# First linear stage of a hybrid diffusion layer: chunk by chunk between sliced adaLN products

## The chip, the cores and the metric
The kernel runs on one core of a Trainium2 chip. The metric is the device time of one execution in microseconds (us). Three runs of the kernel before gave 2493.56, 2496.89 and 2493.85 us, median 2493.85 us.

## The reference
Two layers over 512 latent tokens and 256 context tokens, width 1024, all in float32. Each layer computes, with `c` and `c_ctx` as the two conditions (c is for latent rows, c_ctx for context rows):

```python
mods = split(silu(c) @ w_ada[l] + b_ada[l], 6)        # sh1, sc1, g1, sh2, sc2, g2
h = layernorm(x) * (1 + sc1) + sh1                      # "modulate"
y = token_mixers(h @ w_in[l])                           # attention A, attention B, Fourier C; gates
x = layernorm(ALPHA * x + g1 * y, ln1_g[l], ln1_b[l])
f = swiglu(layernorm(x) * (1 + sc2) + sh2)
x = layernorm(ALPHA * x + g2 * f, ln2_g[l], ln2_b[l])
```

In branch C the columns `uc = h @ w_in[:, uc part]` (512 features) go through a two-dimensional Fourier transform: over the 128 channels of a group, then over the positions.

## The kernel before, in words
The four big engines and the DMA queue of SyncE (SP) run one instruction list each; semaphores order them. The work is a list of phases, written out by `plan()`: first_norm, modulate, fourier_in, then per layer tokens_a, fourier, merge_c, attention (branch A), merge_a, values, attention (branch B), merge_b, and the channel mixer. Every engine walks the phases in this order. Weights come as a stream of units of 512 KB (128 partitions x 1024 columns), double buffered: SP loads a unit in two halves into `raw` (L417) when GpSimd has finished with the unit two before, ScalarE copies it to `w_hi` in a reduced-precision form (L587, `split`), GpSimd subtracts to get `w_lo` (L513, `lo_part`), and TensorE multiplies three terms, w_lo x h_hi, w_hi x h_lo and w_hi x h_hi.

- **first_norm.** SP loads `w_first` (the first 18 x 128 columns of w_ada of layer 0) in eight row blocks of 1152 KB into two buffers (L494). ScalarE's queue loads x (L666), the last two tiles after TensorE has used the first block. TensorE multiplies the conditions with each block (L1717), all eight accumulate in banks 0 to 4; then the rows are copied out (L679) and turned into columns (L1724). VectorE sums x (L1259), finds the inverse root of each of the six token tiles by a chain of eleven small steps (L1155 to L1166), and with ScalarE normalises x into `xn_first` (L1236, L631). When the products are complete and biased (L1110), `mods` for the first modulation are there.
- **modulate.** For each of 8 feature chunks TensorE transposes six tiles of 128 tokens (L1774, two banks each, four chunks in flight), ScalarE scales and shifts (L650), ScalarE or VectorE makes `h_hi` (L656, L1250), VectorE makes `h_lo` (L1244).
- **fourier_in.** Four units, one for 128 output features each, contract all 8 chunks at a time (L1745, L1747); ScalarE copies the result to `u_cols` (L694).
- **tokens_a.** Queries, keys and values of branch A, tokens on the partitions (L1830).
- **fourier.** TensorE multiplies `u_cols` with the channel DFT (L1888) in 12 pieces, ScalarE copies each to `z_sb` (L797). `z_sb` lies over `rope` and over the buffers of the adaLN units, so the first copy waits for `rope_step` (the table `rope_g` is made, L1296) and for `ada_used` of 42 units. Then the position DFT (L1901, L1905), with `mix` made by VectorE (L1355), which afterwards rotates q and k (`rotate`, L1316 to L1339).
- **merge_c.** Twelve units of gates and branch weights; VectorE multiplies a pair of chunks (L1380) after each three units.

The rest of the adaLN columns are made by VectorE in units of 128 columns: SP loads one (512 KB, L425, three buffers, each reload waits until VectorE has used the unit three before), and VectorE runs two multiply-and-sum products of 128x1024 (L1104), one for each condition; a copy of the conditions is loaded first (L430). `ADA_WINDOWS` puts units 18 to 41 ahead of tokens_a (they run beside fourier_in and tokens_a) and 42 to 47 in values; units 48 to 95 run beside the channel mixer. SP has one queue: a load that waits for VectorE holds up the weight loads behind it.

Of the kernel before, what the change touches and what calls it, by code (L numbers as in the profile page):

```python
# [65 lines left out]
ADA_WINDOWS = {("fourier_in", 0): (18, 42), ("values", 0): (42, 48)}  # L66
# [4 lines left out]
ADA_FIRST = 18  # L71
# [105 lines left out]
def increments(ph):  # L177

    t, k = ph.tiles, ph.kind
    if k == "first_norm":  # L180
        return {"loaded": 16 * t, "summed_x": t, "mean_ready": t, "squared": t, "norm_step": SECOND_ROOT * t, "root_ready": t,
                "normed": t // 2, "normed_odd": t // 2}
    if k == "modulate":
        return {"turned": KD, "h_val": KD, "h_hi": KD // 2, "h_hi_odd": KD // 2, "h_lo": KD}
# [18 lines left out]
    if k == "fourier_in":  # L203
        return {"evacuated": 4}
# [25 lines left out]
def build(nc, x_in, ctx_in, cond, cond_cols, w_first, w_ada, b_ada, stream, qk_gain, norm_rows, bias, ident_in,  # L230
# [21 lines left out]
    h_lo = sb("h_lo", [P, KD, TOK], F32R)  # L252
    acc = sb("acc", [P, KD, TOK])
# [71 lines left out]
    ada_at = {"fourier_in": 60, "values": 80, "gate_up": 72}  # L325
    ada_raw = {k: sb(f"ada_raw_{k}", [P, ADA_SLOTS, D], at=R + a * K) for k, a in ada_at.items()}
    ada_cond = {k: sb(f"ada_cond_{k}", [P, 2, D], at=R + (a + 12) * K) for k, a in ada_at.items()}
    ada_unused = {k: sb(f"ada_unused_{k}", [P, D], mybir.dt.bfloat16, at=R + (a + 20) * K) for k, a in ada_at.items()}


    first_raw = sb("first_raw", [P, 2, ADA_FIRST * P], at=R)
    first_rows = sb("first_rows", [2, ADA_FIRST * P], at=R + 48 * K)
    cond_act = sb("cond_act", [P, KD, 2], at=R + 58 * K)
    cond_rows = sb("cond_rows", [2, D], at=R + 60 * K)
# [44 lines left out]
    first_ready = [nc.alloc_semaphore(f"first_ready{s}") for s in range(2)]  # L379
# [27 lines left out]
    with block:  # L407

        @block.sync
        def _(sp):  # L410
# [49 lines left out]
            def window(ph, u):  # L460

                first, end = ADA_WINDOWS[ph.kind, 0]
                step = u - ph.unit - 4
                if step == 0:
                    if ph.kind == "fourier_in":
                        sp.wait_ge(S("h_lo"), KD)
# [3 lines left out]
                for part in (step - 1, step):  # L470
                    n = first + ADA_SLOTS * part
                    if step % 2 == 0 and part >= 0 and n < end:
                        load_ada(ph.kind, n, ADA_SLOTS)
# [15 lines left out]
            sp.dma_start(cond_act[:, :, :], cond_cols[:, :, :]).then_inc(S("cond_loaded"), 16)  # L489
            for k in range(KD):  # L490
                if k >= 2:

                    sp.wait_ge(S("first_used"), k - 1)
                sp.dma_start(first_raw[:, k % 2, :], w_first[k, :, :]).then_inc(first_ready[k % 2], 16)  # L494
            for u in range(n_units):
                for ph in phases:
                    if ph.kind == "bridge":
                        load_rows(ph, u)
                    elif (ph.kind, ph.layer) in ADA_WINDOWS:
# [3 lines left out]
                load_unit(u)  # L503
# [67 lines left out]
        def _(act):  # L571
            prime(act, ("gated", "projected", "silu", "evacuated"))
            consts = [(ident[:, :], ident_in[:, :]),
                      (ada_bias[:, :], b_ada[:, :]), (dft_c[:, :], dft_ch[:, :])]
            act.dma_start(cond_rows[:, :], cond[:, :]).then_inc(S("cond_loaded"), 16)
            act.wait_ge(S("cond_loaded"), 32)
# [81 lines left out]
            def rows_of_input(t):  # L658
# [432 lines left out]
        def _(dve):  # L1091
# [186 lines left out]
            def modulate(ph):  # L1278
                parts_of_h(ph, 0)
# [1235 lines left out]
```

## Time and profile before
| | us |
|---|---|
| median of three runs | 2493.85 |
| the profiled execution | 2498.33 |
| its span (first to last instruction) | 2496.5 |
| TensorE busy | 2315.2 (93%) |
| VectorE busy | 1222.7 (49%) |
| ScalarE busy | 949.3 (38%) |
| GpSimd busy | 1088.3 (44%) |

Matmul ends are modelled, so busy TensorE is not TensorE at its peak. The mean granted clock of TensorE was 0.978 of 2.4 GHz. DMA moved 263.86 MB, 106 GB/s in the mean, 244 GB/s in the first fortieth of the span.

### The profile page before, as it was taken

How to read it: one execution, taken by the hardware profiler on the slowest of the kernel's cores; microseconds unless marked ns; L12 is line 12 of the kernel's file. 1: busy time of each engine (PE TensorE's matmuls, PEld its weight loads, DVE VectorE, ACT ScalarE, POOL GpSimd, SP SyncE). 2: the span in 40 equal slices, each digit the busy share in tenths (PEclk: the TensorE clock that was granted, in tenths of full speed). 3: DMA queues.
4: the chain of work that ended last, by engine and by line, in shares of the span. 5: the costliest groups of instructions: out<-in, count | busy, mean ns of one | idle time of the engine just before them, and what ended most of it. 6: DMA issues, size and time to landing. Idle time of an engine off the chain costs nothing. (4 is left out here: it accounts for less than half of the span.)

```text
span 2496.5 us, 34770 instructions
## 1 busy us (share of the span) xinstructions
PE 2315.2 (93%) x13090; PEld 2107.2 (84%) x13090; DVE 1222.7 (49%) x2548; ACT 949.3 (38%) x1852; POOL 1088.3 (44%) x844
## 2 busy tenths in 40 slices
PE   6989999998899989999999979899998898999997
PEld 2879888987789989999999868778877788988887
DVE  5786266565543474663831274546635526311124
ACT  3222366435541562111111244256535536422223
POOL 1333255434443544333532433446434456644545
PEclk9989999999999999999999989999999999999999
DMA  6541100132112535443522533121222245533335
GB/s 244 193 139 51 51 26 26 43 137 58 58 45 74 181 130 190 134 154 107 171 90 67 161 101 122 54 64 35 65 67 66 66 152 161 152 94 99 110 117 170
DMA packets 117935, 263.86 MB, mean 106 GB/s; under 512 B 13348, under 2 KB 13604, under 8 KB 116136
## 3 DMA queue, kind: packets, MB, share of 16 engines
q1 hardware_dynamic: 108000, 233.89, 29.6%
q10 hardware_dynamic: 9800, 28.19, 3.4%
q8 instruction: 82, 1.34, 0.2%
q14 instruction: 53, 0.43, 0.1%
HBM read 251.53 MB, written 10.49 MB: 105 GB/s over the span
## 5 line engine op out<-in xcount | busy, mean ns | idle before, releaser
L513 POOL TENSOR_TENSOR w_lo<-raw,w_hi 128x512 fp32r<-128x512 f32 x632 | 864.8, 1390 | 1031.2 <-ACT w_hi L587 1030.6
L587 ACT ACTIVATE w_hi<-raw 128x512 fp32r<-128x512 f32 x632 | 366.8, 626 | 682.8 <-PE ps L1747 251.1
L525 POOL TENSOR_TENSOR p_sb<-p_sb,row_inv 128x768 f32<-128x768 f32 (+2 forms) x160 | 185.3, 1168 | 300.7 <-DVE row_inv L1486 300.0
L1745 PE MATMUL ps<-h_hi,w_lo 128*128 128x384 f32 (+1 forms) x864 | 311.4, 360 | 1.2 <-DVE h_lo L1244 1.2
L1745 PE MATMUL ps<-h_lo,w_hi 128*128 128x384 f32 (+1 forms) x864 | 311.1, 360 | 0.0
L1745 PE MATMUL ps<-h_hi,w_hi 128*128 128x384 f32 (+1 forms) x864 | 311.1, 360 | 0.0
L1576 DVE TENSOR_TENSOR ps<-silu_g,ps 128x768 f32<-128x768 f32 (+3 forms) x52 | 37.8, 726 | 379.4 <-PE ps L1747 177.5
L1745 PEld LDWEIGHTS ps<-h_hi,w_lo 128*128 128x128 f32 x864 | 162.2, 188 | 17.3 <-DVE h_lo L1244 1.4
L1745 PEld LDWEIGHTS ps<-h_lo,w_hi 128*128 128x128 f32 x864 | 162.2, 188 | 16.0
L1745 PEld LDWEIGHTS ps<-h_hi,w_hi 128*128 128x128 f32 x864 | 162.2, 188 | 15.9
L2091 PE MATMUL ps<-h_hi,w_lo 128*128 128x384 f32 (+1 forms) x408 | 134.3, 364 | 27.1 <-DVE k_ll L1431 14.8
L1747 PE MATMUL ps<-h_hi,w_hi 128*128 128x384 f32 x456 | 152.3, 334 | 0.0
L1747 PE MATMUL ps<-h_lo,w_hi 128*128 128x384 f32 x456 | 152.3, 334 | 0.0
L1747 PE MATMUL ps<-h_hi,w_lo 128*128 128x384 f32 x456 | 152.3, 334 | 0.0
L870 ACT ACTIVATE pt_hi<-ps 128x512 fp32r<-128x512 f32 (+1 forms) x208 | 114.3, 550 | 97.7 <-PE ps L2036 96.3
L1104 DVE SCALAR_TENSOR_TENSOR ada_unused_gate_up<-ada_raw_gate_up,ada_cond_gate_up 128x1024 bf16<-128x1024 f32 x96 | 143.2, 1491 | 5.3 <-DMA ada_raw_gate_up<-in_w_ada 0.3
L1493 DVE TENSOR_TENSOR pt_lo<-ps,pt_hi 128x512 fp32r<-128x512 f32 (+1 forms) x208 | 129.5, 624 | 21.6 <-ACT pt_hi L870 20.3
L862 ACT ACTIVATE p_sb<-ps,neg_max 128x768 f32<-128x768 f32 (+2 forms) x160 | 120.4, 753 | 35.6 <-DVE neg_max L1479 19.1
L2091 PE MATMUL ps<-h_lo,w_hi 128*128 128x384 f32 (+1 forms) x408 | 132.0, 359 | 0.0
L2091 PE MATMUL ps<-h_hi,w_hi 128*128 128x384 f32 (+1 forms) x408 | 131.9, 358 | 0.0
L2036 PE MATMUL ps<-ident,p_sb 128*128 128x128 f32 x736 | 108.8, 280 | 20.2 <-DVE pt_lo L1493 16.7
L2036 PEld LDWEIGHTS ps<-ident,p_sb 128*128 128x128 f32 x736 | 84.8, 141 | 42.8 <-DVE pt_lo L1493 36.3
(219 smaller groups left out, 5474.4 us busy)
## 6 DMA issues: line engine op xcount, KB each, us to landing
raw<-in_stream SPq DMA_DIRECT2D x632, 256.0 KB, 2.8
ada_raw_gate_up<-in_w_ada SPq DMA_DIRECT2D x48, 512.0 KB, 3.6
ada_raw_fourier_in<-in_w_ada SPq DMA_DIRECT2D x24, 512.0 KB, 4.4
bias_sb<-in_bias ACTq DMA_DIRECT2D x32, 320.0 KB, 3.0
first_raw<-in_w_first SPq DMA_DIRECT2D x8, 1152.0 KB, 5.2
scratch<-xr ACTq DMA_DIRECT2D x16, 512.0 KB, 3.8
xr<-scratch SPq DMA_DIRECT2D x14, 512.0 KB, 4.9
ln_rows<-in_norm_rows SPq DMA_DIRECT2D x8, 512.0 KB, 5.2
```

The lines of the kernel that those rows point to most:

```text
L513: nc.gpsimd.tensor_tensor(w_lo[:, u % 2, cols], raw[:, u % 2, cols], w_hi[:, u % 2, cols].bitcast(F32), ALU.subtract).then_inc(S("lo_made" ...
L525: nc.gpsimd.tensor_tensor(p, p, row_inv[:, c:c + 1].broadcast_to([P, keys]), ALU.mult).then_inc(S("p_ready"), 1)
L587: nc.scalar.activation(w_hi[:, s, cols], raw[:, s, cols], ACT.Copy).then_inc(S("hi_made"), 1)
L862: nc.scalar.activation(p_sb[branch][n % 2][i][:, 0:keys], region(branch, i, 0, keys), ACT.Exp, bias=neg_max[:, i:i + 1], accum_out=row_sum ...
L870: nc.scalar.activation(pt_hi[branch][:, a:a + w], ps[:, TURN_BANK[branch] + order % 2, 0:w], ACT.Copy).then_inc(S("hi_out"), 1)
L1104: nc.vector.scalar_tensor_tensor(ada_unused[kind][:, :], ada_raw[kind][:, s, :], 1.0, ada_cond[kind][:, c, :], ALU.mult, ALU.mult, accum_o ...
L1493: nc.vector.tensor_tensor(pt_lo[branch][:, a:a + w], ps[:, TURN_BANK[branch] + order % 2, 0:w], pt_hi[branch][:, a:a + w].bitcast(F32), AL ...
L1576: nc.vector.tensor_tensor(up, shaped(silu_g[:, c, 0:w]), up, ALU.mult).then_inc(S("hidden"), 1)
L1745: last = nc.tensor.matmul(bank(0), tile, x[:, k, 0:split], start=start, stop=stop)
L1747: last = nc.tensor.matmul(bank(1), tile, x[:, k, HALF:TOK], start=start, stop=stop)
L2036: last = nc.tensor.transpose(ps[:, TURN_BANK[branch] + order % 2, col:col + P], p_sb[branch][n % 2][i][:, a:a + P], ident[:, :])
L2091: last = nc.tensor.matmul(ps[:, bank, 0:b - a], tile, x[:, k, a:b], start=r == 0, stop=r == FILL_STEPS - 1, skip_group_check=True)
```

## The change
- w_first has 16 x 128 columns (shift and scale only) and is laid out in eight slices, one for each feature chunk k: the whole contraction for its 256 columns, 1 MB each, each with a buffer of its own. SP issues x first, then the slices, with weight units 0 and 1 behind slices 1 and 2. The small constants go ahead on ScalarE's queue; the gain is loaded in tokens_a.
- VectorE sums each tile of x as it lands and makes one inverse root for all six tiles.
- Three slices of products are made before x is turned, the fourth behind chunk 0's transposes, the other four inside fourier_in, behind chunks 0 to 3.
- fourier_in goes chunk by chunk: its units hold two chunks x 512 features; for every chunk it adds to six banks (four of 512 latent columns, two with 2 x 256 context columns); the transposes of the next chunk stand ahead of and in the middle of its matmuls, in banks 6 and 7, latent and context apart. All evacuations come at the end.
- The 32 adaLN units 16 to 47: 16 in tokens_a (4 ahead of rope_g, 12 behind it), 16 in merge_c (4, 6 and 6 behind its first three pairs), none in values. SP's loads for them stand ahead of single units, by `ADA_LOADS`. Buffers for tokens_a lie in `acc`, for merge_c in the region of the tables.

```diff
-ADA_WINDOWS = {("fourier_in", 0): (18, 42), ("values", 0): (42, 48)}
+ADA_WINDOWS = {"tokens_a": (16, 32), "merge_c": (32, 48)}
+ADA_LOADS = {"tokens_a": {2: 3, 3: 3, 4: 3, 5: 3, 6: 3, 7: 1}, "merge_c": {3: 3, 7: 2, 8: 3, 9: 2, 10: 3, 11: 3}}
+ADA_AFTER_PAIR = (4, 6, 6, 0)
...
-ADA_FIRST = 18
+ADA_FIRST = 2 * KD
+FIRST_AHEAD = 3
...
@@ sync, window(ph, u)
+                loads = ADA_LOADS[ph.kind]
+                step = u - ph.unit
+                if step not in loads:
+                    return
+                if step == min(loads):
+                    if ph.kind == "tokens_a":
+                        sp.wait_ge(S("first_mods"), KD)
                     else:
-                        sp.wait_ge(S("merged"), at(ph, "merged"))
+                        sp.wait_ge(S("mixed"), at(ph, "mixed"))
                     load_cond(ph.kind)
...
+            for t in range(ALLT):
+                src = x_in[t * P:(t + 1) * P, :] if t < LT else ctx_in[(t - LT) * P:(t - LT + 1) * P, :]
+                sp.dma_start(xr[:, t, :], src).then_inc(x_ready[t], 16)
             for k in range(KD):
-                if k >= 2:
-
-                    sp.wait_ge(S("first_used"), k - 1)
-                sp.dma_start(first_raw[:, k % 2, :], w_first[k, :, :]).then_inc(first_ready[k % 2], 16)
+                sp.dma_start(first_raw[k][:, :, :].rearrange("p a b -> p (a b)"), w_first[k, :, :]).then_inc(first_ready[k], 16)
+                if k in (1, 2):
+                    load_unit(k - 1)
...
@@ scalar
             def first_norm(ph):
                 squares(ph, 0, 1)
-                applied(ph, 0)
+                for i in range(0, ALLT, 2):
+                    first_row_out(i // 2)
+                    act.wait_ge(S("root_ready"), at(ph, "root_ready") + 1)
+                    nc.scalar.activation(xn_first[:, i, :], xr[:, i, :], ACT.Identity, scale=inv_s[:, ALLT + i:ALLT + i + 1],
+                                         bias=shift_s[:, i:i + 1]).then_inc(S("normed"), 1)
                 for s in range(2):
                     split(s, s)
...
             def fourier_in(ph):
+                for j in (2, 3):
+                    unit_done(ph.unit + j, j % 2)
+                for c in range(KB):
+                    nc.scalar.activation(u_cols[:, c, 0:LAT], ps[:, c, :], ACT.Copy).then_inc(S("evacuated"), 1)
...
-                        act.wait_ge(S("ada_used"), PRIME - ADA_FIRST + ADA_WINDOWS["fourier_in", 0][1])
...
@@ vector, merge_c
+                for c in range(KD):
+                    pair(acc[:, c, 0:w], c, 3 * (c // 2) + 3)
+                    if c % 2 and not ph.layer:
+                        ada_units(ph.kind, n, n + ADA_AFTER_PAIR[c // 2])
+                        n += ADA_AFTER_PAIR[c // 2]
...
@@ tensor
+            def first_products(k):
+
+                pe.wait_ge(first_ready[k], 16)
+                if k > FIRST_AHEAD:
+                    pe.wait_ge(S("h_lo"), 2 * (k - FIRST_AHEAD) + 2)
+                for j in range(KD):
+                    last = nc.tensor.matmul(first_sums(k), cond_act[:, j, :], first_raw[k][:, j, :], start=j == 0, stop=j == KD - 1)
+                last.then_inc(S("first_used"), 1)
...
             def fourier_in(ph):
...
+                for k in range(KD):
+                    if k + 1 < KD:
+                        turn_first(k + 1, 0)
+                    if 0 < k < KD - FIRST_AHEAD:
+                        first_turned(FIRST_AHEAD + k)
...
+                    u, kk = ph.unit + k // 2, k % 2
+                    weights_ready(u, kk * 512)
+                    pe.wait_ge(S("h_lo"), 2 * k + 2)
+                    for c in range(KB):
+                        if c == KB // 2 and k + 1 < KD:
...
+                            turn_first(k + 1, 1)
+                        tile = slice(512 * kk + P * c, 512 * kk + P * c + P)
+                        for name in TERMS:
+                            w, x = term(name, u % 2, h_hi, h_lo)
...
+                            nc.tensor.matmul(ps[:, c, :], w[:, u % 2, tile], x[:, k, 0:LAT], start=start, stop=stop, skip_group_check=True)
+                            last = nc.tensor.matmul(ps[:, KB + c // 2, CTX * (c % 2):CTX * (c % 2) + CTX], w[:, u % 2, tile], x[:, k, LAT:TOK],
+                                                    start=start and c % 2 == 0, stop=stop, skip_group_check=True)
+                    if kk:
+                        last.then_inc(S("unit_done"), 1)
+                    if FIRST_AHEAD + 1 + k < KD:
+                        first_products(FIRST_AHEAD + 1 + k)
```

## Rows read from the trace of the kernel before

**Rows 1.** The page, part 1: busy time, share of the span, instructions
```profile
PE 2315.2 (93%) x13090; PEld 2107.2 (84%) x13090; DVE 1222.7 (49%) x2548; ACT 949.3 (38%) x1852; POOL 1088.3 (44%) x844
```
**Rows 2.** TensorE's waits, 66 to 520 us: total, times, longest
```profile
PE ps L1888 <- ACT z_sb L797: 10.5, 1, 10.5
```
**Rows 3.** Timeline of TensorE, 0 to 66 us: start, length, line, count
```profile
6.53 9.99 PE L1717 MATMUL ps<-first_raw,cond_act 128*2 128x512 f32 x20 [6.53 <-DMA first_raw<-in_w_first]
19.24 4.03 PE L1717 MATMUL ps<-first_raw,cond_act 128*2 128x512 f32 x10 [2.72 <-DMA first_raw<-in_w_first]
...
55.39 4.35 PE L1774 MATMUL ps<-ident,xn_first 128*128 128x128 f32 x24 [1.50 <-DVE mods L1110]
60.32 1.87 PE L1774 MATMUL ps<-ident,xn_first 128*128 128x128 f32 x12 [0.58 <-DVE h_lo L1244]
```
**Rows 4.** Windows by stage: length, busy us by engine, clock, DMA share, GB/s
```profile
66.40:100.00 33.60, 33.53 (x193) 33.53 (x194) 20.56 (x25) 8.60 (x15) 12.09 (x6) 1.00 0.48 173
99.90:151.10 51.20, 50.40 (x290) 44.39 (x289) 45.26 (x63) 10.16 (x18) 20.54 (x11) 1.00 0.68 233
150.90:175.10 24.20, 13.69 (x51) 11.20 (x50) 22.41 (x33) 10.17 (x28) 8.98 (x4) 0.72 0.36 125
...
193.20:293.40 100.20, 100.13 (x579) 99.81 (x577) 38.99 (x72) 22.95 (x36) 33.48 (x24) 1.00 0.19 58
```
**Rows 5.** Timelines of TensorE and ScalarE in the channel DFT
```profile
150.89 7.07 PE L1888 MATMUL ps<-dft_c,u_cols 128*128 128x256 f32 x32
...
167.82 5.07 ACT L797 ACTIVATE z_sb<-ps 128x512 f32<-128x512 f32 x10 [12.21 <-issue]
```
**Rows 6.** Timeline of VectorE, 167 to 231 us
```profile
167.77 0.82 DVE L1305 TENSOR_TENSOR rope_t<-tok_a 128x640 f32<-128x640 f32 x1
...
178.28 0.96 DVE L1309 TENSOR_TENSOR v_a<-v_raw,v_a 128x768 fp32r<-128x768 f32 x1
...
229.01 1.82 DVE L1380 TENSOR_TENSOR acc<-gate_c,ps 128x768 f32 x2 [0.44 <-DVE tok_a L1339]
```
**Rows 7.** Windows of the start, columns as in rows 4
```profile
5.00:10.00 5.00, 3.47 (x5) 0.61 (x6) 0.00 (x0) 0.00 (x0) 0.00 (x0) 1.00 0.98 408
...
56.00:58.00 2.00, 2.00 (x12) 2.00 (x11) 0.00 (x0) 0.99 (x2) 0.00 (x0) 0.50 0.44 133
...
60.00:62.00 2.00, 1.55 (x12) 1.27 (x12) 1.82 (x3) 2.00 (x5) 0.00 (x0) 1.00 0.00 0
```
**Rows 8.** VectorE's groups by form, 6 to 66 us: busy, mean ns, idle before
```profile
L1160 DVE TENSOR_SCALAR tmp_s<-std_s,var_s 128x1 f32<-128x1 f32 x18 | 4.9, 273 | 0.7
...
L1250 DVE CAST h_hi<-ps 128x768 fp32r<-128x768 f32 x3 | 2.9, 957 | 3.3 <-ACT ps L650 3.0
```
**Rows 9.** ScalarE's groups by form, 6 to 66 us
```profile
L650 ACT ACTIVATE ps<-ps,mods 128x512 f32<-128x512 f32 x6 | 4.5, 752 | 4.7 <-PE ps L1774 4.7
L631 ACT ACTIVATE xn_first<-xr,shift_s,inv_s 128x1024 f32<-128x1024 f32 x3 | 3.7, 1235 | 5.4 <-DVE shift_s L1166 5.4
L650 ACT ACTIVATE ps<-ps,mods 128x256 f32<-128x256 f32 x6 | 3.2, 540 | 0.0
```
**Rows 10.** Timeline of SP's queue, 66 to 300 us: issues
```profile
88.95 14.10 SPq L425 DMA_DIRECT2D ada_raw_fourier_in<-in_w_ada  x6
```
**Rows 11.** The adaLN products of the first window: min/median/max ns, first and last start
```profile
L1104 DVE SCALAR_TENSOR_TENSOR ada_unused_fourier_in<-ada_raw_fourier_in,ada_cond_fourier_in x48: 1224/1226/2229, 76.6 to 164.1; 128x1024 bf16<-128x1024 f32 x48
...
  DMA ada_raw_fourier_in<-in_w_ada: 13.6, 6
```
**Rows 12.** VectorE's groups, 512 to 536 us (values)
```profile
L1104 DVE SCALAR_TENSOR_TENSOR ada_unused_values<-ada_raw_values,ada_cond_values 128x1024 bf16<-128x1024 f32 x12 | 17.5, 1455 | 7.6 <-DMA ada_raw_values<-in_w_ada 5.6 <-DVE ada_unused_values L1104 1.1
```
**Rows 13.** Tile raw, 193 to 293 us: from issue to landing
```profile
DMA to landing us min/median/max: 2.5/2.6/2.9
```
**Rows 14.** The subtractions to w_lo, 76 to 166 us, columns as in rows 11
```profile
L513 POOL TENSOR_TENSOR w_lo<-raw,w_hi x20: 1291/2248/2357, 76.7 to 157.8; 128x512 fp32r<-128x512 f32 x20
```
**Rows 15.** Window of the adaLN products in values, columns as in rows 4
```profile
512.30:535.30 23.00, 23.00 (x107) 19.41 (x106) 17.61 (x25) 5.08 (x8) 9.89 (x6) 1.00 0.44 156
```

More of the change, by code:

```diff
@@ L460, in window @@
             def window(ph, u):
[L462 to L466, printed above, removed]
+                loads = ADA_LOADS[ph.kind]
[5 more added lines that the diff above has]
+                        sp.wait_ge(S("first_mods"), KD)
                     else:
-                        sp.wait_ge(S("merged"), at(ph, "merged"))
+                        sp.wait_ge(S("mixed"), at(ph, "mixed"))
                     load_cond(ph.kind)
[L470 to L473, printed above, removed]
+                n = ADA_WINDOWS[ph.kind][0] + sum(count for other, count in loads.items() if other < step)
+                load_ada(ph.kind, n, loads[step])
             def beside(ph, u):
@@ new lines, in first_norm @@
+                step = chain("norm_step", at(ph, "norm_step"))
+                var, root, tmp, inv = (x[:, ALLT:2 * ALLT] for x in (var_s, std_s, tmp_s, inv_s))
+                dve.wait_ge(S("squared"), at(ph, "squared") + ALLT)
+                step(nc.vector.tensor_scalar(var, square_s[:, 1, :], 1.0 / D, EPS, ALU.mult, ALU.add))
+                step(nc.vector.tensor_scalar(tmp.bitcast(I32), var.bitcast(I32), 1, None, ALU.logical_shift_right))
+                step(nc.vector.tensor_scalar(inv.bitcast(I32), tmp.bitcast(I32), -1.0, ROOT_SEED, ALU.mult, ALU.add))
@@ new lines, in first_norm @@
+                for turn in range(3):
+                    step(nc.vector.scalar_tensor_tensor(tmp, inv, -0.5, inv, ALU.mult, ALU.mult))
+                    step(nc.vector.tensor_tensor(tmp, tmp, var, ALU.mult))
+                    step(nc.vector.scalar_tensor_tensor(inv, tmp, 1.5, inv, ALU.add, ALU.mult))
+                dve.wait_ge(S("mean_ready"), at(ph, "mean_ready") + ALLT)
+                nc.vector.tensor_tensor(shift_s[:, :], neg_mean[:, 1, :], inv, ALU.mult).then_inc(S("root_ready"), 1)
@@ L1290, in tokens_a @@
                     dve.wait_ge(S("stored"), at(ph, "stored"))
+                else:
+                    dve.wait_ge(S("cond_loaded"), 16 * 3)
+                    first, end = ADA_WINDOWS[ph.kind]
+                    ada_units(ph.kind, first, first + 4)
+                    dve.wait_ge(S("gain_loaded"), 16)
                 step = chain("rope_step", at(ph, "rope_step"))
@@ L1299, in tokens_a @@
                 step(last)
+                if not ph.layer:
+                    ada_units(ph.kind, first + 4, end)
+                    ada_biased(first, end, 1)
                 dve.wait_ge(S("evacuated"), at(ph, "evacuated") + ph.tiles + ALLT)
```

252 lines of the change are left out of this document (128 added, 124 removed).

## The prediction, on record before the change was run
> **What bounds the kernel now.** I read the page's totals first: TensorE is busy 93% of the span [rows 1], so a change gains only where TensorE stands still or where its work is not dense. The chain that ended last reaches back 27 us only and says nothing of the start. The waits of TensorE behind the first stage, to 520 us, hold one large entry: 10.5 us at L1888, the channel DFT, for ScalarE's copies to z_sb [rows 2]. The timeline of the first 66 us shows TensorE doing adaLN products at the pace of their transfers, some transposes, and no dense work before 66.5 us [rows 3]. The stages by windows [rows 4]: fourier_in to 100.0 us, tokens_a to 151.05, the DFT over channels to 175.05 (the position DFT behind it starts there), merge_c from 193.2 to 293.3. The window 150.9:175.1 is the hole: 24.2 us with 13.7 busy and a clock of 0.72, because the z_sb copies start at 167.82 [rows 5], after VectorE has worked off 24 adaLN units (the last product starts at 164.1, [rows 11]) and built rope_g (done ahead of 167.77, [rows 6]).
>
> So two places can pay: the 66.5 us ahead of fourier_in, and that hole.
>
> **The start.** Before, first_norm needs all of w_first (9.4 MB) ahead of any mods. Now x goes first, then slices of 1 MB. 5:10 moved 408 GB/s [rows 7]. With about 1 MB moved by 5 us, the 3.4 MB of x and constants are in at about 11 us and seen at 12; slice 0 is seen at 14.5, slice 1 at 17, slice 2 (unit 0 ahead of it) at 21, slice 3 (unit 1) at 24.7, the rest each 2.6 us later.
> Roots: of the six chains one is left, on six columns: thirteen steps of at most 0.27 us and 0.04 between [rows 8], 3 to 4 us. x summed at 14.6, squared at 16, root at 19. That is not the limit; the products are. Ten matmul records of a 2304-column row took 4.03 us at the full clock, while the first twenty took 9.99 [rows 3], about 5 us of them at half pace. A slice is 8 x 256 columns: 4.03 x 2048/2304 = 3.6 us, the first 6. So slice 0 ends at 20.5, 1 at 24.1, 2 at 27.7. ScalarE takes its three normalised tiles between the row copies, each behind first_used, so the last one (1.24 us, [rows 9]) ends at 29.4, though the root was there at 19. Transposes of chunk 0 to 31.1; slice 3 to 34.7; fourier_in proper begins at 35.5.
>
> Each chunk k then costs TensorE: matmuls 33.6/8 = 4.2 (same columns as before: [rows 4], 512+256 for 384+384), six transposes 1.75 (twelve records in 1.87, [rows 3]), 0.3 for the small transposes and semaphores; and chunks 0 to 3 a slice of products, 3.6. Four at 9.8, three at 6.1, the last at 4.2: 61.7. End at about **97**, against 100.0. Gain 3 us: the head start of 31 us is nearly eaten by 18 us of products and 14 of transposes that now stand in the dense stream, and by its own first chunk.
> Does one PSUM buffer for two chunk parts stall it? A part's round trip is ScalarE 0.75 (512) or 0.54 (256) [rows 9], then VectorE twice, at most 0.96 each (for 768 columns, [rows 8]). For the 256 part that is about 1.7 us, under 2.1 us of matmuls and the next 1.15 of transposes. I take 0; the other end is 8 x 1 us.
>
> The interleaved transposes could cost clock. At 56:58 the granted clock was 0.50 (1.2 GHz); TensorE did nothing but transposes from 51.8 us on [rows 3], and at 60:62 it was 1.00 (2.4 GHz) [rows 7]. So they brought it up themselves, and I charge nothing. The Trainium skill says the opposite ("TensorE: Matmul & The Clock Gate", Part 4: PE-mode transpose: transposes don't count as TensorE being busy, and the full clock does not engage for them); this trace does not agree with it, and its case is rival D.
>
> **tokens_a.** 51.05 us before, with 0.8 not busy (its window, [rows 4]), the wait for w_lo whose weights SP had issued late, between adaLN loads: six of them took 14.1 us to issue [rows 10]. Now the loads are spread over its steps and the queue keeps ahead. New: six evacuations at its start, behind a split; the tile of bank 0 is needed 1.4 us in and free at 1.9: +0.5. Net -0.3. Ends at 97 + 50.8 = 147.9.
> VectorE here: h_lo ends at 92.5; 24 units took 76.6 to 165.3 less 7.5 of waiting for transfers between them (13.6 in all, 6.1 of it ahead of the first, [rows 11]), 3.38 a unit. Four units to 106; gain and rope, issued behind the evacuations, give rope_g at 109; twelve more to 150. ScalarE's tokens are out at 150.4. So VectorE is just not late, and the z_sb gate (rope_g) was open long before.
>
> **The hole.** Twelve z of 0.88 us (eight in 7.07 us before the stop, [rows 5]) are 10.6 us, ScalarE's 12 copies at 0.51 [rows 5] start at 152.6 and end with them. 24.0 becomes 10.6: **-13.4**. VectorE's squares take 178.28 + 0.96 - 167.77 = 11.5 us [rows 6], to 162; the first odd part is there at 158.5 + 4.6 + 0.6 = 163.7. What is late next is the products themselves. The position DFT takes 18.2 as before; merge_c begins at **M = 176.7** instead of 193.2: 16.5 earlier.
>
> **merge_c with 16 units.** VectorE ends the rotation and takes the first pair 35.8 us after M (229.01 - 193.2, [rows 6]), 1.8 for a pair; pairs are ready from TensorE at M+24.9, 49.8, 74.7, 99.6. A unit took (1.455 + 0.15) x 2 = 3.2 us in values, where weights are split as here [rows 12]. Units 32 to 35 end at M+50, 36 to 41 at M+71, 42 to 47 at M+95.6; pair 3 is in time. But SP issues weight unit u behind loads that wait for ada_used three units back. Step 8 waits for adaLN unit 36 (M+55.3), step 9 for 38 (61.7), step 10 for 41 (71), step 11 for 44 (M+86.2); then the load lands in 2.6 us [rows 13], here with a 512 KB load ahead, is copied (0.6) and subtracted on GpSimd (1.3 alone, 2.2 beside products): 5.8 to 6.7 in all [rows 14]. Needed at M+66.4, 74.7, 83, 91.3. The first three hold; the last comes at about M+92.7: **+1.4** (0 to 3 with this unit price). Behind it stand only unit 22 and 23, needed 8 us later.
> The same unit price has another end: a product took 1.22 to 2.23 us, median 1.23 [rows 11], so a unit is between 2.8 and 4.5.
> The window in values goes: 24 us of VectorE there, and 3.5 MB. TensorE was 23.00 busy of 23.00 us in it [rows 15], so it was covered: 0 (below it -1, from transfers). The shift of mods_ready, unrolled loops and one more adaLN sum at the end of merge_c (0.2 us in a 2.0 us wait): 0 each, at most 0.5.
>
> **Sum**: -3.0 - 0.3 - 13.4 + 1.4 = -15.3, rounded -15. The profiled execution took 2498.33 us, span 2496.5 and 1.8 outside, 4.5 above the median of the three runs, 2493.85. Its sum would be 2483; the same difference on the median gives **2479**.
>
> **Rivals.**
> A. The start gives nothing or costs (transfers slower than 408 GB/s, more products at half pace, round trips of chunks not covered: up to 8): fourier_in ends at 101 to 106, so 2483 to 2488. For: the step from 29 to 35 us hangs on five engines in turn. 15%.
> B. The start gives 6 to 10 (transposes run beside matmuls, products slot in): 2470 to 2474. 12%.
> C. The other side: SP's queue. Products run at their long form, 2.08 us, all the time, a unit of 4.46. Then VectorE ends the first window at 166, its squares at 177, M becomes 180 (-13); in merge_c unit 36 ends at M+63.7, 41 at M+86, 44 at M+101, and steps 8, 10 and 11 wait 4.3, 5.7 and 7 us for weights: +17. Net +4: **2498**. It decides from about 4.2 us a unit on. Against: median 1.23. 6%; half of it (3.8 a unit, +8 in merge_c), 2487: 6%.
> D. The transposes hold the clock at 1.2 GHz through the interleaved stage. At the low level a matmul takes twice its time, as the first products did [rows 3]; the 33.6 us of matmuls would take as much again, and products and transposes some 15: 2528. 2%. (This is the rule of the page named above.)
> E. The hole is not closed but moved: something else holds the z_sb copies, or gains drain in attention behind (TensorE waits there for VectorE in its own rhythm). 2490 to 2495. 5%.
> The forecast itself, 2474 to 2484, 54%.
>
> **Numbers.** A measurement of this kernel tells 0.2% from nothing, 5 us. Faster: 54 + 12 + 15 x 0.85 + 5 of C's half = 84%. Same: rest of A, most of E: 8%. Slower: C and D, 8%. The range reaches from B's better end to A and half of C: 2469 to 2490.
>
> **What would show it.** fourier_in's last matmul at 97 (92 to 102); no wait of TensorE for z_sb, the DFT over channels in 10.6 us; merge_c from 177 on; a wait for w_lo of 0 to 3 us in merge_c's last unit and none in its eighth to tenth; VectorE's product at 1.4 to 1.6 us in the mean. Wrong it is if the first stage's chunks take over 10 us each, if SP's queue delays several units of merge_c, or if the time in values moves.

## The result, and the profile after

| | before | after |
|---|---|---|
| median on the chip of the comparison, us (four runs each) | 2494.49 | 2472.82 (2471.78 to 2477.76) |
| the profiled execution, us | 2498.33 | 2473.38 |
| its span, us | 2496.5 | 2471.3 |

The ratio is 0.9914, with a 95% interval of 0.9899 to 0.993: 0.86% faster. The forecast was 2479 in a range of 2469 to 2490. The median fell by 21.7 us, the profiled span by 25.2; by the stages read below the change itself is worth 23 us up to the start of attention.

The totals of the page of the changed kernel (for [rows 1]). TensorE is busy 4.6 us less and the span is 25.2 us shorter: what went is mostly time in which it stood still.

```profile
PE 2310.6 (93%) x13136; PEld 2106.0 (85%) x13136; DVE 1223.4 (50%) x2530; ACT 948.0 (38%) x1853; POOL 1085.4 (44%) x844
```

Windows by stage of the changed kernel, columns as in [rows 4] (length; busy time and count of TensorE, its weight load, VectorE, ScalarE, GpSimd; clock, DMA share, GB/s): the stream of fourier_in, tokens_a, the DFT over channels, the one over positions, merge_c.

```profile
35.00:89.30 54.30, 54.30 (x305) 39.37 (x304) 20.80 (x37) 13.87 (x24) 8.53 (x6) 1.00 0.25 86
89.20:140.60 51.40, 51.06 (x291) 44.65 (x290) 49.45 (x64) 12.87 (x24) 23.32 (x12) 1.00 0.71 238
140.40:150.80 10.40, 10.40 (x51) 9.15 (x50) 8.94 (x13) 9.56 (x26) 3.30 (x2) 1.00 0.01 2
150.80:169.00 18.20, 18.20 (x98) 15.70 (x96) 8.01 (x26) 3.57 (x6) 3.62 (x2) 1.00 0.00 0
168.90:270.00 101.10, 100.10 (x579) 99.78 (x577) 88.00 (x136) 23.13 (x35) 42.07 (x24) 1.00 0.47 156
```

The line to read first is 140.40:150.80: the DFT over channels is 10.4 us, all busy, at a clock of 1.00, against 24.2 with 13.7 busy and a clock of 0.72 [rows 4]. The stream of fourier_in is busy in all of its 54.3 us too, so whatever is cheaper there than forecast is cheaper work, not a wait that closed. merge_c has 88.0 us of VectorE in it, 39.0 before, and TensorE lost 1.0 us to that.

The start, timeline of TensorE:

```profile
14.72 13.13 PE L1761 MATMUL ps<-first_raw,cond_act 128*2 128x256 f32 x48 [14.72 <-DMA first_raw<-in_w_first]
27.78 0.81 PE L1768 MATMUL ps<-ident,first_rows 2*128 2x2 f32 x6
29.45 0.88 PE L1823 MATMUL ps<-ident,xn_first 128*128 128x128 f32 x6 [0.85 <-ACT xn_first L689]
30.25 3.61 PE L1761 MATMUL ps<-first_raw,cond_act 128*2 128x256 f32 x16
34.33 0.28 PE L1768 MATMUL ps<-ident,first_rows 2*128 2x2 f32 x2 [0.46 <-ACT first_rows L682]
34.54 0.65 PE L1823 MATMUL ps<-ident,xn_first 128*128 128x128 f32 x4
34.95 0.48 PE L1891 MATMUL ps<-h_hi,w_lo 128*128 128x512 f32 x1
```

The third row prices a chunk: its six transposes take 0.88 us. The last shows the dense stream starting at 34.95 (forecast 35.5).

The hole, timeline of VectorE, then of ScalarE (for [rows 5, 6]):

```profile
141.57 0.19 DVE L1132 TENSOR_TENSOR mods<-mods,ada_bias 128x32 f32<-128x32 f32 x1
142.88 0.82 DVE L1349 TENSOR_TENSOR rope_t<-tok_a 128x640 f32<-128x640 f32 x1 [1.11 <-ACT v_raw L749]
```
```profile
143.56 0.95 ACT L760 ACTIVATE v_a<-v_raw 128x768 fp32r<-128x768 f32 x1
144.30 4.70 ACT L815 ACTIVATE z_sb<-ps 128x512 f32<-128x512 f32 x9
149.26 0.60 ACT L815 ACTIVATE z_sb<-ps 128x512 f32<-128x512 f32 x1 [0.27 <-PE ps L1969]
```

VectorE is through its adaLN units 1.1 us before its first tokens come. ScalarE copies z_sb 3.9 us after the DFT began and ends waiting for TensorE, not the other way round. The wait of 10.5 us [rows 2] is gone. The wait that was forecast to come in its place, for the weights of merge_c's last unit, is this row of TensorE's waits (total, times, longest):

```profile
PE ps L1797 <- POOL w_lo L534: 1.0, 1, 1.0
```

| stage | before | forecast | after | forecast gain | measured gain |
|---|---|---|---|---|---|
| fourier_in ends (tokens_a begins) | 99.9 | 97 | 89.2 | 3.0 | 10.7 |
| tokens_a, length | 51.0 | 50.8 | 51.2 | 0.3 | -0.2 |
| DFT over channels, length | 24.2 | 10.6 | 10.4 | 13.4 | 13.8 |
| merge_c begins | 193.2 | 176.7 | 168.95 | 16.5 | 24.3 |
| attention begins | 295.45 | | 272.23 | 15.3 | 23.2 |

Behind the start of attention the two kernels run the same code, but for the six adaLN units that the kernel before makes in values and the way the sums of the adaLN units are closed. There the difference between the two profiles moves on from 23.2 to 25.2; the last experiments show how large such drift is in a kernel that isn't changed at all.

### The profile page after: what moved, and what is told of

Read it like the earlier page. It is cut to its first block and busy times, and to the rows that moved or that the text cites. A ratio compares the mean times of both kernels' runs of the same rounds, so it can differ in the third digit from the quotient of the medians.

```text
span 2471.3 us, 34690 instructions
## 1 busy us (share of the span) xinstructions
PE 2310.6 (93%) x13136; PEld 2106.0 (85%) x13136; DVE 1223.4 (50%) x2530; ACT 948.0 (38%) x1853; POOL 1085.4 (44%) x844
## 5 line engine op out<-in xcount | busy, mean ns | idle before, releaser
L1797 PE MATMUL ps<-h_hi,w_lo 128*128 128x384 f32 (+1 forms) x832 | 300.6, 361 | 0.0
L1797 PE MATMUL ps<-h_lo,w_hi 128*128 128x384 f32 (+1 forms) x832 | 300.4, 361 | 0.0
L1797 PE MATMUL ps<-h_hi,w_hi 128*128 128x384 f32 (+1 forms) x832 | 300.4, 361 | 0.0
L1797 PEld LDWEIGHTS ps<-h_hi,w_hi 128*128 128x128 f32 x832 | 156.2, 188 | 16.0
L1797 PEld LDWEIGHTS ps<-h_hi,w_lo 128*128 128x128 f32 x832 | 156.2, 188 | 15.8
L1797 PEld LDWEIGHTS ps<-h_lo,w_hi 128*128 128x128 f32 x832 | 156.2, 188 | 15.8
L2172 PE MATMUL ps<-h_hi,w_lo 128*128 128x384 f32 (+1 forms) x408 | 134.9, 366 | 27.1 <-DVE k_ll L1483 14.8
L1799 PE MATMUL ps<-h_hi,w_hi 128*128 128x384 f32 x424 | 141.6, 334 | 0.0
L1799 PE MATMUL ps<-h_lo,w_hi 128*128 128x384 f32 x424 | 141.6, 334 | 0.0
L1799 PE MATMUL ps<-h_hi,w_lo 128*128 128x384 f32 x424 | 141.6, 334 | 0.0
L1543 DVE TENSOR_TENSOR pt_lo<-ps,pt_hi 128x512 fp32r<-128x512 f32 (+1 forms) x208 | 129.5, 624 | 21.9 <-ACT pt_hi L888 20.6
L2172 PE MATMUL ps<-h_hi,w_hi 128*128 128x384 f32 (+1 forms) x408 | 132.6, 360 | 0.0
L2172 PE MATMUL ps<-h_lo,w_hi 128*128 128x384 f32 (+1 forms) x408 | 132.5, 360 | 0.0
## 6 DMA issues: line engine op xcount, KB each, us to landing
first_raw<-in_w_first SPq DMA_DIRECT2D x8, 1024.0 KB, 18.2
```

The lines of the kernel that those rows point to most:

```text
L1543: nc.vector.tensor_tensor(pt_lo[branch][:, a:a + w], ps[:, TURN_BANK[branch] + order % 2, 0:w], pt_hi[branch][:, a:a + w].bitcast(F32), AL ...
L1797: last = nc.tensor.matmul(bank(0), tile, x[:, k, 0:split], start=start, stop=stop)
L1799: last = nc.tensor.matmul(bank(1), tile, x[:, k, HALF:TOK], start=start, stop=stop)
L2172: last = nc.tensor.matmul(ps[:, bank, 0:b - a], tile, x[:, k, a:b], start=r == 0, stop=r == FILL_STEPS - 1, skip_group_check=True)
```

## The experiments

The ratios are to the kernel before, run on the same chip. A time "above the changed kernel" is a difference of medians from its 2472.82; the changed kernel measured once more gave 2475.9 (changed_again), so such a difference is good to some 3 us. "Shift" is how much later GpSimd makes the low part of a given weight unit than in the changed kernel's profile: it reads a stage without what happens behind it. In changed_again it is -0.4 us through the first stages, so a shift of a few tenths is no effect.

**The hole, half undone in the kernel before.**
```diff
-ADA_WINDOWS = {("fourier_in", 0): (18, 42), ("values", 0): (42, 48)}
+ADA_WINDOWS = {("fourier_in", 0): (18, 39), ("values", 0): (39, 48)}
```


> The kernel before with three adaLN units fewer in the first window (18 to 38) and nine instead of six in values; nothing else. Theory: the hole in the channel DFT is VectorE's window, at 3.38 us a unit. It then ends near 155 instead of 165.3, the z_sb copies start near 158 instead of 167.8, and the position DFT starts near 164 instead of 175.1: 10 to 11 us off the time (2483 to 2485), nothing lost in values (nine units are 29 us, the stage is 49). Rival: ScalarE's copies wait for something else (tokens, dft tables), then the copies start later than 162 and under 5 us are gained.

2488.62 us, ratio 0.998 (0.9966 to 0.9993). TensorE's waits, 100 to 300 us:

```profile
PE ps L1888 <- ACT z_sb L797: 2.1, 1, 2.1
```

Three adaLN units fewer, and 10.5 us of waiting became 2.1. The copies to z_sb start at 160.1, and all that is behind is 9.1 us earlier than in the kernel before by the weight units. So the cause of the hole is shown: VectorE's adaLN units of the first window, at about 3 us each, where 3.38 and 10 to 11 us in all were expected. The medians give 6.5 of the 9.1.

**The hole, put back into the changed kernel.**
```diff
-ADA_WINDOWS = {"tokens_a": (16, 32), "merge_c": (32, 48)}
-ADA_LOADS = {"tokens_a": {..., 7: 1}, "merge_c": {3: 3, 7: 2, 8: 3, 9: 2, 10: 3, 11: 3}}
-ADA_AFTER_PAIR = (4, 6, 6, 0)
+ADA_WINDOWS = {"tokens_a": (16, 40), "merge_c": (40, 48)}
+ADA_LOADS = {"tokens_a": {..., 7: 6, 8: 3}, "merge_c": {3: 3, 7: 2, 8: 3}}
+ADA_AFTER_PAIR = (4, 4, 0, 0)
```


> The changed kernel with 24 adaLN units in tokens_a (12 loads more) and 8 in merge_c. rope_g is still made behind the first four, so the gate of z_sb stays open. Theory: what matters is how many units VectorE has to do there, gate or not: it ends near 168 instead of 141.6, its squares and the first mix come at 181 to 182 instead of 156, and merge_c starts near 184 instead of 169: 13 to 16 us slower than the changed kernel (about 2487). The channel DFT itself keeps its 10.4 us. Rival: the gate alone made the hole; then under 4 us slower.

2483.25 us, ratio 0.9958, 10.4 above the changed kernel; TensorE begins merge_c 9.3 us later, and the shift is about +9 behind merge_c. Both steps of the expectation failed. The first: the DFT over channels did not keep its 10.4 us. Its waits (TensorE), then SP's queue and ScalarE:

```profile
PE ps L1969 <- ACT z_sb L815: 6.2, 1, 6.2
```
```profile
131.69 15.22 SPq L443 DMA_DIRECT2D ada_raw_tokens_a<-in_w_ada  x6
146.95 0.91 SPq L435 DMA_DIRECT2D raw<-in_stream  x2
```
```profile
150.90 1.28 ACT L608 ACTIVATE w_hi<-raw 128x512 fp32r<-128x512 f32 x2 [8.32 <-DMA raw<-in_stream]
152.09 0.83 ACT L760 ACTIVATE v_a<-v_raw 128x768 fp32r<-128x768 f32 x1
152.82 5.04 ACT L815 ACTIVATE z_sb<-ps 128x512 f32<-128x512 f32 x10
```

Here it is not the gate on `ada_used` (it is gone) that holds z_sb but the queues: six loads that wait for VectorE took SP until 146.91, the weight unit behind them came late, ScalarE waited 8.32 us for it in order to split it, and the z_sb copies stood behind that split. With the wait, and the clock that fell with it (next row), the DFT over channels took 19.8 us, from 140.2 to 160.1.

```profile
153.00:163.00 10.00, 9.55 (x31) 7.79 (x32) 9.54 (x15) 6.06 (x12) 2.09 (x1) 0.67 0.46 158
```

The second: VectorE's lateness by itself cost TensorE nothing up to here. VectorE worked on adaLN units to 164.0 and on its squares to 175.8, and `mix` stands behind both; the low part of merge_c's first weights, which GpSimd makes behind it, came 12.5 us later. But the position DFT took its 18.2 us as in the changed kernel, and TensorE's timeline shows merge_c's first product right behind it, with no wait (168.95 in the changed kernel):

```profile
178.22 0.42 PE L1797 MATMUL ps<-h_hi,w_lo 128*128 128x384 f32 x1
```

So the 9.3 us are all the channel DFT's. The same 24 units on VectorE find two different ways to the same place, z_sb.

**SP's queue in merge_c.**
```diff
-"merge_c": {3: 3, 7: 2, 8: 3, 9: 2, 10: 3, 11: 3}
+"merge_c": {3: 3, 7: 2, 8: 3, 9: 2, 10: 6}
```


> The changed kernel with the last three adaLN loads of merge_c (45 to 47) one step earlier in SP's queue, ahead of weight unit 20 instead of 21. The last waits for unit 44, which VectorE ends only behind pair 2. Theory: SP's order is what a weight unit waits for; unit 20 is issued near 255 instead of 240.7, its w_lo is there near 261, while TensorE wants it at 252: 8 to 11 us slower than the changed kernel (2481 to 2484), with a wait for w_lo of that size and the 1.0 us wait at the last unit gone. Rival: there is slack in the buffers; under 2 us.

2480.63 us, ratio 0.9947, 7.8 above the changed kernel. SP's queue, then TensorE's waits:

```profile
233.25 20.62 SPq L443 DMA_DIRECT2D ada_raw_merge_c<-in_w_ada  x6
253.92 21.11 SPq L435 DMA_DIRECT2D raw<-in_stream  x9
```
```profile
PE ps L1797 <- POOL w_lo L534: 8.9, 1, 8.9
```

In the changed kernel SP issues the same six loads in two parts of three, with weights between them:

```profile
233.27 7.39 SPq L443 DMA_DIRECT2D ada_raw_merge_c<-in_w_ada  x3
240.71 0.91 SPq L435 DMA_DIRECT2D raw<-in_stream  x2
250.15 5.54 SPq L443 DMA_DIRECT2D ada_raw_merge_c<-in_w_ada  x3
```

Behind one another they keep SP for 20.6 us, and TensorE waits 8.9, as expected. What the forecast charged with 1.4 (measured 1.0) is this mechanism, and the distance between 1 and 9 is one entry of a table.

**What a transpose in the stream costs.**
```diff
-                for t in range(a // P, b // P):
+                for t in [*range(a // P, b // P)] * 2:
```


> The changed kernel with each transpose of the first stage issued twice in a row (the same result written twice). It prices the transposes. Theory: one record is one transpose, 0.145 us in a stream, 0.87 for the six of a chunk: 7 us slower than the changed kernel (about 2480), and fourier_in ends near 96 instead of 89.3. Rival (the price in my prediction): 1.75 a chunk, 14 us slower; then the 7.7 us by which fourier_in ended earlier than forecast came from elsewhere.

2479.1 us, ratio 0.9932. The shift behind fourier_in is +4.97 us and stays so to merge_c. TensorE's groups by form, 28 to 90 us in the changed kernel, then 28 to 96 in this one (count, busy, mean ns):

```profile
L1823 PE MATMUL ps<-ident,xn_first 128*128 128x128 f32 x48 | 8.0, 279 | 0.9 <-ACT xn_first L689 0.9
```
```profile
L1823 PE MATMUL ps<-ident,xn_first 128*128 128x128 f32 x96 | 13.3, 276 | 0.8 <-ACT xn_first L689 0.8
```

48 more transposes cost 4.97 us: 0.62 for the six of a chunk, 0.10 for one. The forecast had 1.75 for a chunk, which would have made 14 us; the expectation had 0.87 and 7 us, still too much, since it took the price from six transposes in a row (0.88), and between matmuls they cost less.

**What a product in the stream costs.** The products of slices 3 to 7 are issued twice over.
```diff
-                for j in range(KD):
-                    last = nc.tensor.matmul(first_sums(k), ...)
+                for turn in range(2 if k >= FIRST_AHEAD else 1):
+                    for j in range(KD):
+                        last = nc.tensor.matmul(first_sums(k), ...)
```


> The changed kernel with the products of slices 3 to 7 issued twice over (same sums, 16 records for 8 in each). My sum charges a slice in the stream with its full 3.6 us, so five more slices cost 18 us: fourier_in ends at 107.3 in place of 89.3, the time is 2491. The rival, by which the products slot into waits of the stream for ScalarE and VectorE (and the first stage was shorter than forecast for that reason), expects under 8 us: 2473 to 2481. What is behind the stage should keep its length either way.

2490.31 us, ratio 0.9984; the shift behind fourier_in is +17.7, or 3.5 us a slice for five slices. The stream has no gaps in which products would hide: what TensorE is given there it pays in full. The forecast's 3.6 us for a slice holds.

**x behind the slices.** The loop that loads x stands behind the one that loads the slices.

> The changed kernel with x transferred behind all eight slices and units 0 and 1. It shows what the transfer order gives without the rest of the change. By the measured rate of 410 GB/s the slices and units are in at 27 us and x at 31 to 32; VectorE keeps up with the transfers, root at 35 to 36, tiles at 40, first large transpose at 40 in place of 29.45. Theory: everything behind is 10 to 11 us later, 2483. The rival, that the start is bound by the products, by which x could come at any time up to some 28 us, expects under 3 us.

2491.04 us, ratio 0.9983; the shift is +17.7, more than the 10 to 11 expected. ScalarE's first normalised tile:

```profile
40.66 1.24 ACT L689 ACTIVATE xn_first<-xr,shift_s,inv_s 128x1024 f32<-128x1024 f32 x1 [2.39 <-DVE shift_s L1300]
```

Two things make up the difference. The root is there at 40.7 where 35 to 36 was expected: the first tile of x is seen at 28.75, but the six are not in by 31 to 32. Transfers run to 34 us, VectorE's six sums, 1.3 us apart, end at 36.6, ScalarE's squares at 38.0. From the root to the first large transpose it is 4.1 us, as expected (40 from 35 to 36), so that one is at 44.7. The second is the clock, for TensorE had by then stood still for most of 25 us; windows of this kernel and its timeline of TensorE:

```profile
23.00:44.00 21.00, 1.08 (x6) 0.86 (x6) 12.20 (x28) 11.05 (x18) 0.00 (x0) 0.50 0.54 218
44.00:49.00 5.00, 4.25 (x13) 1.99 (x14) 1.84 (x6) 3.84 (x7) 3.71 (x4) 0.50 0.20 55
```
```profile
44.74 1.54 PE L1823 MATMUL ps<-ident,xn_first 128*128 128x128 f32 x6 [0.76 <-ACT xn_first L689]
46.22 5.36 PE L1761 MATMUL ps<-first_raw,cond_act 128*2 128x256 f32 x16
```

The clock of the second window is 0.50, and the transposes and the slice take 1.54 and 5.36 us in place of 0.88 and 3.61: 2.4 us for the clock, beside the 15.3 by which the transposes begin later. So x first, against x last, is worth 17.7 us by itself: with x last the changed kernel would be hardly faster than the kernel before.

**ScalarE's order.** The three normalised tiles ahead of the second and third row copy.
```diff
+                first_row_out(0)
                 for i in range(0, ALLT, 2):
-                    first_row_out(i // 2)
...
+                for k in range(1, FIRST_AHEAD):
+                    first_row_out(k)
```


> The changed kernel with ScalarE's three normalised tiles ahead of its copies of the second and third row of products. Theory: the chain that starts fourier_in is TensorE's third slice (27.8), the row copy, and then the third normalised tile (28.2 to 29.4). With the tiles done by 25.3, what is left is the row copy and the small transposes: the first large transpose at 28.5 instead of 29.45, everything 0.9 us earlier, 2472. Rival: slice 3's arrival or the mods are later than that, and nothing moves.

2476.33 us (2469.07 to 2479.16), ratio 0.9916 (0.9895 to 0.9938). TensorE's timeline, for the row at 29.45 above:

```profile
14.96 13.42 PE L1763 MATMUL ps<-first_raw,cond_act 128*2 128x256 f32 x48 [14.96 <-DMA first_raw<-in_w_first]
28.31 0.81 PE L1770 MATMUL ps<-ident,first_rows 2*128 2x2 f32 x6
29.06 0.88 PE L1825 MATMUL ps<-ident,xn_first 128*128 128x128 f32 x6
```

The wait of 0.85 us for the tile is gone and the chain is 0.9 shorter behind the products, but these ended 0.5 later in this execution, so the shift is -0.4, which changed_again has without any edit. At the end of the span it is +5.8. The step is read from the trace alone, and is too small to be seen in the time.

**Transposes ahead of the products.** TensorE turns `ident` 16 times before it waits for the first slice.
```diff
+                pe.wait_ge(S("consts"), 16 * 3)
+                for n in range(16):
+                    nc.tensor.transpose(ps[:, 5, P:2 * P], ident[:, :], ident[:, :])
...
-                pe.wait_ge(S("consts"), 16 * 3)
```


> The changed kernel, and TensorE turns the identity matrix 16 times into an unused part of PSUM from about 9.3 us on, while it waits for the first slice (seen at 14.7). In the changed kernel the first slice's products took 6.1 us and each later slice 3.6, though the granted clock of both stretches reads 1.00. If transposes bring TensorE to its full pace, as the kernel before seems to show at 51.8 to 58.5 us, the first slice now takes about 3.6 to 4.0 us and fourier_in's stream starts where the third normalised tile lets it, about 1.5 to 2 us earlier, since slice 2 ends at 25.4 in place of 27.8: time 0 to 2 us below the changed kernel's 2472.8. If transposes do not count as work for the clock (the rival), the first slice stays at 6.1 us and the time is unchanged.

2471.74 us (2469.6 to 2473.17), ratio 0.9905 (0.9888 to 0.9921). Timeline of TensorE, then windows of the first slice in this kernel and, last, of the changed kernel in the first of these stretches:

```profile
9.27 3.62 PE L1775 MATMUL ps<-ident 128*128 128x128 f32 x16 [9.27 <-DMA dft_c<-in_dft_ch]
14.89 12.21 PE L1761 MATMUL ps<-first_raw,cond_act 128*2 128x256 f32 x48 [2.00 <-DMA first_raw<-in_w_first]
```
```profile
14.80:16.10 1.30, 1.21 (x6) 0.53 (x7) 1.27 (x3) 1.23 (x3) 0.00 (x0) 1.00 1.01 422
16.20:19.40 3.20, 3.20 (x9) 1.03 (x8) 1.79 (x6) 2.48 (x4) 0.00 (x0) 0.50 1.04 412
```
```profile
14.80:16.10 1.30, 1.30 (x4) 0.38 (x3) 1.27 (x3) 1.23 (x3) 0.00 (x0) 1.00 1.01 419
```

The mechanism of the expectation is right, and its gain is not there. In the first stretch six product records fit, where the changed kernel has four: the first slice begins at the full clock, and TensorE had done nothing but the 16 transposes by then. So transposes do raise the clock, as [rows 7] let the prediction say. But TensorE had waited 2.0 us for the slice after them, and from 16.2 to 19.4 us the clock is down at 0.50, with nine records in 3.20 us. So three slices took 12.2 us in place of 13.1, not 10.8, and the shift is -0.8. In changed_again the three slices took 12.7 without any edit, so only about half of that can be put down to the transposes.

**Slices 0 and 1 ahead of x**, on top of ScalarE's order.
```diff
+            for k in range(2):
+                sp.dma_start(first_raw[k][:, :, :].rearrange("p a b -> p (a b)"), w_first[k, :, :]).then_inc(first_ready[k], 16)
             for t in range(ALLT):
...
-            for k in range(KD):
-                sp.dma_start(first_raw[k][:, :, :].rearrange("p a b -> p (a b)"), w_first[k, :, :]).then_inc(first_ready[k], 16)
+            for k in range(1, KD):
+                if k > 1:
+                    sp.dma_start(first_raw[k][:, :, :].rearrange("p a b -> p (a b)"), w_first[k, :, :]).then_inc(first_ready[k], 16)
```


> The same order on ScalarE, and slices 0 and 1 transferred ahead of the six tiles of x. In the changed kernel VectorE takes the tiles of x at 1.3 us each from 9.5 us on, because it waits for the constants first, so x may come up to 4 us later at no cost. Theory: products of slices 0 and 1 from about 7 to 17 us, slice 2 seen at about 21 as before and done by 25; root at 21.5 to 23; the third tile at 25.3 to 26.7; first large transpose at 25.5 to 27 in place of 29.45, then slice 3: the dense stream starts 2.5 to 4 us earlier, 2469 to 2470.5. Rival: slice 3 (seen at 24.7) and then the mods hold it, or x's later arrival moves the root by the 5 us that the two slices take, and the gain is under 1 us.

2473.9 us (2468.34 to 2477.52), ratio 0.9914 (0.9894 to 0.9935). Timeline of TensorE and windows:

```profile
6.32 10.01 PE L1766 MATMUL ps<-first_raw,cond_act 128*2 128x256 f32 x32 [6.32 <-DMA first_raw<-in_w_first]
21.00 6.04 PE L1766 MATMUL ps<-first_raw,cond_act 128*2 128x256 f32 x16 [4.68 <-DMA first_raw<-in_w_first]
```
```profile
16.40:21.00 4.60, 0.00 (x0) 0.00 (x0) 3.15 (x8) 4.06 (x8) 0.00 (x0) 0.80 1.03 406
21.00:27.00 6.00, 6.00 (x17) 1.76 (x17) 3.95 (x14) 3.77 (x4) 0.00 (x0) 0.59 1.03 425
```

The shift is -1.75, not -2.5 to -4. The products began 8.4 us earlier and slice 2, which landed only at 21.0, still ended at 27.0, because in the pause of 4.7 us before it the clock fell: slice 2 took 6.04 us in place of 3.6, at a clock of 0.59. The Trainium skill describes this ("TensorE: Matmul & The Clock Gate", HAM oscillation: a wait for a transfer between groups of matmuls drops the clock and the next group starts slow); the trace agrees, with 2.4 us for one pause.

**Three slices ahead of x**, slice 3 ahead of the transposes, and the changed kernel itself beside it on the same chip. The diff of the first is in SP's loop (x behind slice 2, units 0 and 1 behind slice 3), in ScalarE's first_norm (the copies of rows 0 to 2 ahead of the normalised tiles) and in TensorE's modulate:
```diff
+                first_products(FIRST_AHEAD)
                 pe.wait_ge(S("normed"), at(ph, "normed"))
                 pe.wait_ge(S("normed_odd"), at(ph, "normed_odd"))
                 for c in range(2):
                     turn_first(0, c)
-                first_products(FIRST_AHEAD)
```


> Slices 0, 1 and 2 are transferred ahead of x, slice 3 behind x and ahead of weight units 0 and 1, TensorE does the products of slice 3 ahead of the first large transposes, and ScalarE copies rows 0 to 2 ahead of the normalised tiles. Theory: TensorE's products run without the pause of 4.7 us that slices_first showed (and so without the second slow slice of 6.0): 6.3 to 12.3, 16, 19.6, and slice 3, seen at about 21, to 24.6. x lands by about 18, VectorE ends its sums at 19, root at 22 to 23, tiles at 26.5, first large transpose at 26.6 and, with nothing between it and the dense stream but one chunk's way through ScalarE and VectorE, the stream starts at 29.5 to 31 in place of 34.95: 4 to 5.5 us off, about 2468. Rival: the first chunk's way and the weights of unit 0 (their low part was made at 30.0 in the changed kernel) hold it, and under 2 us comes off.

> The changed kernel as it is, on the same chip and in the same rounds as the next one, so that the two can be compared. Expected: 2472 to 2474, ratio to the kernel before 0.991 to 0.992.

slices_before_x: 2474.59 us (2465.22 to 2479.29), ratio 0.9911 (0.9895 to 0.9928). changed_again: 2475.9 us (2470.69 to 2480.07), ratio 0.9916 (0.9903 to 0.9929). The shift of the first is -1.1, which is the number of the rival (under 2 us), and mostly for another reason than the rival gave. Timeline of TensorE:

```profile
6.34 13.10 PE L1764 MATMUL ps<-first_raw,cond_act 128*2 128x256 f32 x48 [6.34 <-DMA first_raw<-in_w_first]
22.99 0.81 PE L1771 MATMUL ps<-ident,first_rows 2*128 2x2 f32 x6 [3.56 <-ACT first_rows L684]
23.73 6.03 PE L1764 MATMUL ps<-first_raw,cond_act 128*2 128x256 f32 x16
```

The pause has only moved: the row copies stood behind ScalarE's squares, TensorE stood still for 3.6 us, and slice 3 took 6.03, so the first large transpose came at 29.7 and not at 26.6. No version beats the changed kernel by more than its own spread.

That spread is the second thing this pair shows. changed_again is the changed kernel word for word. Its profile lies 0.4 us ahead of the first one through unit 36 and is 6.8 longer at the end. The two differ in windows such as this one, of the first and then of the second execution:

```profile
525.00:534.00 9.00, 6.95 (x42) 6.95 (x43) 5.96 (x17) 6.48 (x14) 4.80 (x4) 1.00 0.20 60
```
```profile
525.00:534.00 9.00, 7.31 (x33) 7.31 (x34) 5.68 (x16) 6.12 (x13) 4.79 (x4) 0.81 0.20 60
```

The same work, 42 matmul records in one and 33 in the other, at a clock of 1.00 and 0.81; between units 36 and 42 the second falls 2.6 us behind. That is in attention, where TensorE waits often for VectorE. Why the clock falls in one execution there and not in the other stays open.

## Why the prediction was right, point by point

- **What bounds the kernel.** Right: by the start of merge_c the changed kernel is 24.3 us ahead, from the start (10.7) and from the hole (13.8), the two places that were named.
- **The start.** The mechanism was right, the size was not. First large transpose 29.45 against a tile at 29.4; stream from 34.95 against 35.5. Then the stream took 54.3 us in place of 61.5, and the step that failed is "six transposes 1.75 (twelve records in 1.87, [rows 3])". The twelve records were taken for the transposes of one chunk. A group of 48 records over all eight chunks, as the changed kernel shows it, says one record for a transpose: twelve are two chunks. The kernel before could have told this; its 24, 12 and 12 records of L1774 are those same 48. Charged at 0.62 to 0.88 in place of 1.75, seven chunks are 6.1 to 7.9 us cheaper, which holds the 7.2 that the stream was shorter by. The sum has a small slip besides: its own terms give 9.85 and 6.25 us for a chunk, where 9.8 and 6.1 were added, so it should read 62.4 and not 61.7. Against that the stream is 8.1 us shorter, and what the transposes leave of it, 0.2 to 2, lies in terms that no run priced by itself, such as the 0.3 us for small transposes and semaphores. The other terms held: 3.5 to 3.6 for a slice (products_twice), nothing for one buffer of PSUM with two parts (the stream is busy in 54.30 of the window's 54.30 us).
- **The clock under transposes.** Clock 1.00 in the stream: rival D is out, and the charge of nothing was right. So was its reason: in transposes_ahead 16 transposes alone brought the clock up.
- **tokens_a.** 51.2 us for 50.8. The wait of 0.8 is gone, one of 0.3 for ScalarE's evacuations came. It ends at 140.4 for 147.9, which is the start's doing. VectorE was through its units at 141.8, 1.1 us ahead of its tokens, where 150 and 150.4 were forecast: just not late, by a little more than thought.
- **The hole.** -13.8 for -13.4, the copies from 144.30, that is 3.9 us behind the end of tokens_a for 4.7. Rival E, another gate on the copies, did not happen here; after_24_8 shows that it stood close by. That run also shows that VectorE's squares and `mix`, which the prediction followed to 163.7, could be late without TensorE waiting for them.
- **merge_c.** First pair at 204.30, 35.35 us behind its start, for 35.8. Wait for weights 1.0 for 1.4, in the last unit. VectorE's products 1.53 us in the mean (49.0 us for 32), inside the 1.4 to 1.6. Rival C, 2.1 us a product, is out.
- **The sum.** -15.3 was forecast for the start of attention, -23.2 measured. Put 7.7 more into the first term and the sum is -23.0. So rival B's numbers, 2470 to 2474, were the ones that came, by a mis-sized term and not by products that slot into gaps. B's other reason, transposes beside matmuls, is true in a small part: a transpose costs 0.10 us in the stream and 0.15 in a row of six. The number 2479 was 6.2 us too high, and the range held because it reached down to B. How much of the start's gain comes from the order chunk by chunk and how much from the sliced products was not run apart.
- **The window in values.** Its removal is worth what the drift hides: the difference of the two profiles stays at 23.0 there. Covered, as forecast.

## What to carry to other kernels

Before a row is taken as a price, find out how many program instructions its count stands for: compare the total count of the line with its loop in the code. Look for units of work of one engine that are finished just before a gate, and count them off against idle room further on; three units moved were 8.4 us of a wait. Then look at what each moved unit does to queues it passes, since the same units held the same copies a second time through SP and a weight split.

## What the runs showed of the hardware

- An early start is worth less if it opens a pause. With a pause of 4.7 us or 3.6 us between products, the next slice took 6.0 us in place of 3.6, about what the very first slice of the changed kernel takes (6.2).
- Transposes alone raise TensorE's clock. Behind 16 of them the first six product records took 1.21 us of TensorE's time where the changed kernel has four in 1.30 (transposes_ahead); a wait of 2.0 us stood between, and the window at 0.50 begins only behind 16.1 us.
- The first slice in the changed kernel took 6.2 us (14.7 to 20.9) though its window shows a clock of 1.00:

```profile
14.70:20.90 6.20, 6.18 (x17) 1.96 (x18) 4.45 (x17) 3.87 (x8) 0.00 (x0) 1.00 1.01 406
20.90:27.80 6.90, 6.90 (x34) 2.57 (x31) 2.70 (x6) 3.12 (x4) 0.00 (x0) 1.00 1.04 426
```

  17 records in 6.2 us and then 34 in 6.9: ahead of the first change of clock that the profile records, the pace of the records tells the clock and the column does not.
- Identical kernels differ by 7 us in two profiled executions, and stretches of low clock in attention account for a part of it (2.6 us between units 36 and 42). A gain of 1 or 2 us at the start can be read in the trace at its stage, and can't be read in the time.
